# A two-layer hybrid decode step on one core: states and new values written beside the output products, cache copies at other places, squares of norms in another buffer

## The reference, cut

```python
for l in range(DEPTH):                              # DEPTH = 2, D_MODEL = 1024
    xn = rms_norm(x, norm_w[l])                     # prompt (256) and sample (8 x 4) tokens: 288 columns
    q_a,k_a,v_a,g_a,qi,ki,wi,q_c,k_c,v_c,g_c,z,xbc,dt = split(xn @ w_in[l])
    o_a = sparse attention: indexer scores over 2048 cached keys + new ones, top 256, softmax, values (paged cache)
    o_c = dilated window attention, windows 128/512/2048, dilations 1/4/16
    y_b, conv_new, h_new = Mamba-2 SSD: causal conv, chunked scan, gated RMSNorm; h_new is the new state
    x = x + concat[o_a * silu(g_a), o_c * silu(g_c), y_b] @ w_out[l]
    new buffers: dil_g = concat(cache_dil_g, new rows)[4:]     # the old rows are copied, shifted by 4
y = rms_norm(x, final_norm_w)
# returned too: new k/v/ki rows, conv tails, states p_ssd and s_ssd, window buffers of every sequence
```

## Time and profile before

| | |
|---|---|
| median of 3 runs | 586.1 us (583.58 to 590.11) |
| the profiled execution, its own time | 584.74 us |
| its span, first to last instruction | 583.1 us |
| mean granted clock of TensorE | 0.993 |
| PE busy | 555.4 us (95%) |
| VectorE, ScalarE, POOL busy | 355.3, 176.2, 238.7 us |
| moved by DMA | 198.37 MB in 75252 packets, mean 340 GB/s |
| layer 0 / layer 1 on PE | 6.9 to 291.9 / 291.9 to 574.3 us |

### The profile page before, as it was taken

The page is one execution under the profiler, slowest core; times in us unless marked ns, Lnnn a source line. Parts: engine busy times, 40 slices in busy tenths (PEclk is TensorE's granted clock), DMA queues, the critical chain, the costliest instruction groups (busy, mean ns, idle before and its releaser), DMA issues.

```text
span 583.1 us, 13433 instructions
## 1 busy us (share of the span) xinstructions
PE 555.4 (95%) x4656; PEld 385.4 (66%) x4656; DVE 355.3 (61%) x1085; ACT 176.2 (30%) x457; POOL 238.7 (41%) x430
## 2 busy tenths in 40 slices
PE   5999999999999999999999999999999999989993
PEld 3776656577777666667777665557777766756762
DVE  4864646576786696443258564657688678843324
ACT  4013512212223615641001252321123182455210
POOL 0505733449423746261111275314873174635200
PEclk9999999999999999899999999999999999999998
DMA  8988999999996999997979999999999699999993
GB/s 340 329 286 284 371 370 377 413 362 355 370 392 200 350 355 367 328 352 266 400 236 375 310 371 370 368 406 411 332 361 387 245 329 355 365 368 316 318 387 134
DMA packets 75252, 198.37 MB, mean 340 GB/s; under 512 B 11601, under 2 KB 44530, under 8 KB 71090
## 3 DMA queue, kind: packets, MB, share of 16 engines
q1 hardware_dynamic: 53138, 98.32, 47.9%
q0 software_dynamic: 21472, 98.03, 46.0%
q10 hardware_dynamic: 576, 1.18, 0.6%
HBM read 189.33 MB, written 52.00 MB: 414 GB/s over the span
## 4 chain that ended last, share of the span: by engine, by line
PE 73%; DMA 17%; SPq 3%; DVE 2%; issue 2%; ACT 2%; POOL 1%; POOLq 0%; DVEq 0%; ACTq 0%
PE bank L956 71%; DMA kv<-in_kk 7%; DMA kv<-in_vv 5%; DMA w<-in_w 5%; SPq L438 2%; PE bank L1002 2%; ACT shared L745 1%; DVE xn L2259 1%; DVE shared L1787 0%; DVE shared L1802 0%; DVE st L1792 0%; POOL kv L438 0%; DVE rstd L1615 0%; ACT pt L899 0%; SPq L434 0%
## 5 line engine op out<-in xcount | busy, mean ns | idle before, releaser
L956 PE MATMUL bank<-xn,w 128*128 128x288 f32 x1120 | 295.2, 418 | 6.9 <-DMA w<-in_w 6.9
L956 PEld LDWEIGHTS bank<-xn,w 128*128 128x128 f32 x1120 | 207.6, 192 | 76.9 <-issue 21.6
L438 POOL DMA_DIRECT2D kv<-in_kk x128 | 68.8, 538 | 90.2 <-issue 44.4
L438 POOL DMA_DIRECT2D kv<-in_vv x128 | 68.9, 539 | 88.1 <-issue 48.0
L698 ACT ACTIVATE pt<-bank 128x288 f32<-128x288 f32 x48 | 19.7, 410 | 180.3 <-PE bank L956 180.3
L956 PE MATMUL bank<-pt,w 128*128 128x288 f32 x256 | 65.2, 409 | 1.3 <-DMA w<-in_w 1.3
L956 PEld LDWEIGHTS bank<-pt,w 128*128 128x128 f32 x256 | 47.8, 190 | 17.0 <-DMA w<-in_w 4.0
L541 POOL DMA_DIRECT2D out_keep<-in_buf x48 | 24.9, 525 | 69.1 <-PE bank L956 67.3
L1698 DVE TENSOR_SCALAR_CACHE_REDUCE hit<-sc,tb 128x516 bf16<-128x516 f32 x62 | 46.5, 750 | 2.2
L956 PE MATMUL bank<-kv,pt 128*32 128x256 f32 x512 | 33.5, 388 | 4.6 <-DMA kv<-in_vv 4.5
L956 PE MATMUL bank<-kv,qz 128*32 128x256 f32 x512 | 34.3, 385 | 0.0
(11 more groups left out here) (262 smaller groups left out, 736.4 us busy)
## 6 DMA issues: line engine op xcount, KB each, us to landing
w<-in_w SPq DMA_DIRECT2D x86, 512.0 KB, 8.1
out_keep<-in_buf POOLq DMA_DIRECT2D x16, 2044.0 KB, 13.9
kv<-in_kk SPq DMA_DIRECT2D x128, 160.0 KB, 8.1
kv<-in_kk POOLq DMA_DIRECT2D x128, 160.0 KB, 5.8
kv<-in_vv SPq DMA_DIRECT2D x128, 128.0 KB, 5.3
kv<-in_vv POOLq DMA_DIRECT2D x128, 128.0 KB, 5.2
kv<-in_dil SPq DMA_DIRECT2D x16, 576.0 KB, 11.7
kv<-in_dil POOLq DMA_DIRECT2D x16, 576.0 KB, 8.3
```

What stands on the lines that cost most here:

```text
L438: engine.dma_start(kv[:, s, r * rec:(r + 1) * rec], a["kk" if what == "page" else "vv"][bass.ds(page + layer * N_POOL, 1)].rearrange("o p ...
L956: return pe.matmul(out, lhsT, rhs, start=start, stop=stop, skip_group_check=True, **k)
```

## The change

1. The squares and their sum go to `shared`. ScalarE's wait for the state's write (`h_out`) moves from the end of each layer to the first Relu of the next layer's index scores. POOL's clearing of the window columns waits in addition for the sum of squares.
2. In the value stretch POOL no longer stops for the writes of the states and of the new values; both are issued after the layer's last ring item, just ahead of the output copies. Their waits go with them.
3. A copy can be split: WHOLE (all windows), SMALL (the first two), LARGE (the third). The total stays. Layer 0 gets a LARGE copy at product 6; each layer a LARGE copy at product 25; the output copies become (whole 5 at `out0`; small 4 and small 7 at `out4`) in layer 0 and (whole 5 and 6 at `out0`; small 4 at `out2`) in layer 1. At the front of layer 1 still two whole sequences are copied, the second of them now layer 1's.

```diff
-FRONT_KEEPS = ((), ((0, 6, "proj1"), (0, 7, "proj4")))
-STAGE_KEEPS = (((0, 0), (0, 1), (0, 2), (0, 3)), ((1, 0), (1, 1), (1, 2), (1, 3)))
-OUTPUT_KEEPS = (((0, 4, "out0"), (0, 5, "out4")), ((1, 4, "proj34"), (1, 5, "proj34"), (1, 6, "out0"), (1, 7, "out1")))
+WHOLE, SMALL, LARGE = (0, 1, 2), (0, 1), (2,)
+FRONT_KEEPS = (((0, 7, LARGE, "proj6"),), ((0, 6, WHOLE, "proj1"), (1, 7, WHOLE, "proj4")))
+STAGE_KEEPS = tuple(tuple((L, b, LARGE if b == 4 else WHOLE) for b in range(5)) for L in range(DEPTH))
+OUTPUT_KEEPS = (((0, 5, WHOLE, "out0"), (0, 4, SMALL, "out4"), (0, 7, SMALL, "out4")),
+                ((1, 5, WHOLE, "out0"), (1, 6, WHOLE, "out0"), (1, 4, SMALL, "out2")))
...
-        squares = prelu
-        sqsum = phasedf[:, 0:T]
...
+        squares = shared[:, 0:8, :].rearrange("p (a t) n -> p a (t n)", a=2)
+        sqsum = shared[:, 8:11, :].rearrange("p t n -> p (t n)")[:, 0:T]
...
                     if u == 3:
+                        pool.wait_ge(S["ssum_ready"], nth(L, "ssum_ready", 1))
                         pool.memset(qcz, 0.0).then_inc(S["qcz_zero"], 1)
...
                 masked(0)
                 masked(1)
+                keep(*STAGE_KEEPS[L][4], "proj25")
                 consumed(*RING[40:44])
                 for t in range(3):
                     y_gated(t)
-                consumed(*RING[44:60])
+                consumed(*RING[44:])
                 pool.wait_ge(drained(f"ss{NB - 1}"), nth(L, f"ss{NB - 1}"))
                 pool.dma_start(a["s_ssd"][ly].rearrange("o p a n -> (o p) a n"), state[:, :, :]).then_inc(S["h_out"], 16)
                 pool.dma_start(a["p_ssd"][ly].rearrange("o p n -> (o p) n"), hfin[:, :]).then_inc(S["h_out"], 16)
-                consumed(*RING[60:64])
                 pool.wait_ge(drained(f"proj{VA + 1}"), nth(L, f"proj{VA + 1}"))
                 feat(VA, VA + 2, 3)
                 feat(VC, VC + 3, 8)
-                consumed(*RING[64:])
...
+                    elif n == 0 and L:
+                        act.wait_ge(S["h_out"], nth(L - 1, "h_out", 32))
...
-                act.wait_ge(S["h_out"], nth(L, "h_out", 32))
-
                 act.activation(warm[:, :], eps[:, :], ACT.Sqrt).then_inc(chain.next(), 1)
```

More of the change, by code:

```diff
@@ L535, in _, with keep @@
                 ly = bass.ds(L, 1)
-                def keep(layer, b, use):
+                def keep(layer, b, groups, use):
                     pool.wait_ge(filled(use), nth(L, use))
-                    for g in range(3):
+                    for g in groups:
                         pool.dma_start(a[f"keep{g}"][bass.ds(layer, 1), b], a[f"buf{g}"][bass.ds(layer, 1), b, 4 * 256:],
@@ L552, in consumed @@
                         after(pool, POOL, L, item)
-                for layer, b, use in FRONT_KEEPS[L]:
-                    keep(layer, b, use)
+                for layer, b, groups, use in FRONT_KEEPS[L]:
+                    keep(layer, b, groups, use)
                 for u in range(NPAIR):
@@ L644, in _ @@
                 feat(VC, VC + 3, 8)
-                consumed(*RING[64:])
-                for layer, b, use in OUTPUT_KEEPS[L]:
-                    keep(layer, b, use)
+                for layer, b, groups, use in OUTPUT_KEEPS[L]:
+                    keep(layer, b, groups, use)
                 for name in ("ki_out", "feat_out", "tail_out", "h_out"):
```

## The result

The changed kernel took 592.0 us, median of 22 runs (585.3 to 598.3), against 587.6 us (582.1 to 593.6, also 22 runs) of the kernel before. The ratio is 1.0082, 95% interval 1.0058 to 1.0106: 4.8 us slower. The forecast was 4.1 us faster, with a range of 578 to 588. The profiled execution was one of the long ones: 594.97 us, span 593.2 against 583.1.

The account below looks back on a forecast made before the run. PE was taken as the bound, busy 555.4 of 583.1 us. The terms -5.67 + 1.1 + 0.2 + 0.3 + 0 = -4.1 us turned the profiled 584.74 into 580.6, or 582.0 for the median, range 578 to 588.

Parts of the forecast that it names:

- Output products of layer 0: Layer 0 outputs: fewer copy bytes nearly cancel the added states and new values; +0.3 us, at most 4.0.
- The value stretch: Both layers: without state and new-value writes, waits of 2.09 and 2.01 us and 1.57 of slow clock go; 5.67 us gained.
- The front of layer 0: Large copy after product 6: what does not fit in DMA room arrives at the page wait of 78.78; +1.1 us.
- rival A: Front of layer 0: the copy starves page loads, costing 5.7 us plus 1.57 for the clock; median 588.2, chance 0.12.
- Behind product 25: Large copy in both layers: the DMA hole from 176 to 183.5 nearly holds it; +0.1 us a layer, 0.2 in all.
- Outputs of layer 1: Layer 1 output products: load on the late weights as before, the stretch ahead lighter; 0 us (-0.5 to +0.5).
- Buffers: Squares and their sum in another buffer, with the waits moved for it: no cost, 0 us.
- B: Value stretch: the wait moves to the next group and the clock drops as before; -0.4 us, median 585.7, chance 0.26.
- C: Whole kernel: front copy costs 0, remaining value waits and 1.3 us of weight waits go too; -7.4, median 578.7, chance 0.16.
- signs of being wrong: Value-group wait over 1.5 us, page waits beyond 4 or clock falling there, or output weights awaited over 2 a layer.

Follow-up runs that it names:

- e0: The changed kernel once more, no edit: 592.0 us, ratio to the kernel before 1.0126.
- e4: Changed kernel, but in layer 0 POOL waits for SP's four page loads for layer 1 before issuing the state write: 583.4 us, ratio 0.9987.
- e5: Changed kernel with the state written in rows of 1.5 KB in place of 12 KB: 588.6 us, ratio 1.0070.
- e2: Changed kernel with states and new values issued in the value stretch again, copies and buffers as changed: 587.5 us, ratio 1.0054.
- e9: Kernel before with only the large copy of sequence 7 moved from the front of layer 1 to that of layer 0: 587.0 us, ratio 1.0010.
- e1: Changed kernel without the copy at the front of layer 0 (sequence 7 copied whole at out4): 589.5 us, ratio 1.0083.
- e6: Changed kernel without the front copy of layer 0 and with page loads landed before the state write: 582.0 us, ratio 0.9956.
- e12: Second run of the changed kernel without the layer 0 front copy and with page loads ahead of the state write: 581.0 us, ratio 0.9926.
- e8: Changed kernel without the layer 0 front copy, states and new values back in the value stretch; copies behind product 25 stay: 585.4 us, ratio 1.0035.
- e7: Kernel before with only the squares in the other buffer and the state-write wait moved to the next layer: 585.4 us, ratio 0.9982.
- e3: Changed kernel with copies at their places of before; only states, new values and squares' buffer moved: 592.3 us, ratio 1.0128.
- e11: Copies where they were, states and new values beside the outputs, page loads ahead of the state write in layer 0: 586.9 us, ratio 1.0011.

## Why the prediction was wrong

**The step that failed is "Output products of layer 0": "The bytes nearly cancel: +0.3".** It came to +8.8: 6.8 us of wait where two waits of together 0.5 had been, and 2.9 of slow clock (+7.1 in e0). Its upper bound, 4.0, was also too low. The account in bytes was right in itself: e4 moves the same bytes at the same outputs, PE does not wait, and the stretch is 0.8 shorter than before. What it left out is who stands in which queue at 268 us. The order rows showed the state write directly behind POOL's last page load, and the weights landed behind the page loads of their own queue (283.3 and 278.8); so the last of SP's twelve page transfers, 1.3 KB rows, would meet 12 KB rows, and the weights asked for next stand behind them. I had the turn by packets in the text, and set it against the front of layer 0 and the value stretch; I did not run it through the seam, the one place where the change brings the longest rows. By the packets it can be worked out, as an estimate from the rows' lengths: at equal turns of 1.3 and 12 KB SP gets a tenth of the 1.5 MB that 369 GB/s move in four us, 0.14 MB, where it had 0.44 (measured: 0.19), so the last pages and thus the weights come several us late. The hole of 2.8 us that I credited lay behind the page loads; now the state write fills it (the shares of the queues from 268 to 272 add to 1.05) and the pages run on through it. How much of the delay is the length of the rows and how much the mere presence of the write at that moment stays open: e5, in one profile, took about half of the wait away.

**The value stretch.** The mechanism was right, and the size too large. I had 5.67; the marks give 2.7 + 0.9 = 3.6 (3.0 in e0). The waits of 2.09 and 2.01 went and so did the slow clock of 1.57. SP's value loads came back from a median of 7.7 to 4.2 us (issued 214 to 236). But what is late next was not priced: PE now waits 0.81 us in each layer for VectorE's prompt probabilities (line 1843), which stood in the shade of the value wait, and other value waits of 0.30 and 0.65 stand where 0 and 0.38 were. 5.67 less 1.62 less 0.57 is 3.5.

**The front of layer 0.** +1.1 forecast. The page waits of layer 0 grew by 1.2 in the changed kernel, 1.7 in e0, 1.3 in e2, 0.8 in e4 and 0.3 in e9. The term holds on the average of the waits, and the first hole is filled as forecast (share 0.47 before, 0.84 now). What it lacked is the clock: one wait of 2.67 us cost another 2.9, and the stretch grew by 3.9. In e2, with the same copy, a wait of 2.54 left the clock whole and the stretch grew by 1.3; in e9, in pieces of at most 0.70, by 0.5. I had that in rival A alone. In time, taking the copy away gave 2.5 us (e1 against e0), 1.8 and 3.6 (e6 and e12 against e4), none of them measured closely enough to tell 1.1 from 4.

**Behind product 25.** +0.2 forecast. In the changed kernel 0.30 and in e0 1.68 us of wait stood at 202 us, e8 leaves -0.4 to +4.5 us. But waits of 0.23 (e7) and 0.41 (e9) stand there without the copy too. The hole is filled (from 176 to 187 us the share is 1.01, before 0.51). Not refuted, not well measured.

**Outputs of layer 1.** Forecast 0; -1.3 in the profile, -1.7 in e0. The copies that left made room for the states. e3 and e11 show what it costs if they don't leave: a wait of 4.6 us.

**Buffers.** Forecast 0, e7 agrees within its interval.

**The tail** grew by 1.3 us. From the last sum of squares to VectorE's last instruction both traces take 6.9 us; the growth stands behind it. The last packets of the copies are through before 585 us, ahead of the first part of y, sent at 586.7, so they are not what the end waits for. The cause is open.

**The rivals.** A came in part: the clock fell among the pages, as its sign said, but the stretch lost 3.9 us (3.3 in e0) where A needs 5.2, and the larger loss stands elsewhere. Neither B nor C came. Of the signs of being wrong, two came: the clock among the pages, and weights waited for over 2 us at the outputs of layer 0. No rival put the loss at the seam, and the bound of 4.0 us for it was too low, so the range ended at 588.

## What to carry to other kernels

In this kernel two DMA queues that were both backed up shared by packets rather than by bytes (175 to 170 packets, 1.51 to 0.19 MB): before a write with long rows is placed, list what stands in the other queue at that moment, how short its rows are, and what stands behind those in the same queue. Here a prefetch that nobody needs for 60 us stood ahead of weights needed in 6; waiting for the prefetch to land before issuing the long write took the loss of 0.8% away (e4: 0.9987, no difference from before), and with the front copy left out as well it became a gain of 0.4 to 0.7%. When a wait is removed, look for the releaser that was in its shade, and price a long single wait of PE with the slow clock that may follow it (2.9 us behind 2.67, nothing behind 2.54).

## What was not expected of the hardware

From 268 to 272 us POOL's queue moved 1.51 MB in 175 packets beside 0.19 MB in 170 on SP's: the turns are equal to 3%, while the bytes stand 8 to 1. With rows of 1.5 KB in the program it was 1.14 to 0.38 MB; there POOL's queue moved 287 packets of 4 KB on the average, so a packet is not a row. The turns are not equal everywhere: 271 to 395 before, 287 to 336 in e5.

The clock does not follow the length of a stand alone. It fell around stands of 2.67 us (changed kernel), 2.20 (e0 and e5), 2.27 (e3) and 2.37 (e9), and held through 2.85 (e7), 2.54 (e2), 2.20 and 2.38 (e8).
